# Attention pairs between the weight pieces of the second projections, heads normalised by token

## The chip, the cores and the metric

The kernel runs on one core of a Trainium2 chip. The metric is the device time in microseconds of one execution. A core has TensorE (PE in the profile, its weight loads PEld), VectorE (DVE), ScalarE (ACT), GpSimd (POOL) and SyncE (SP), which here issues all transfers. Each engine runs its own program in order; semaphores join them. The times before are 2862.55, 2863.42 and 2865.28 us.

## What is computed

Two transformer-like blocks on one sequence of 256 tokens with 2048 channels, in fp32. The change touches only the middle of the second block:

```
h = rms_norm(x, norm1_g)
aq, ak, av, bu, bg, cq, ck, cv = split(h @ w_in)      # 512 x 5, 1024, 128, 128 columns
aq, ak, cq, ck: rms_norm over each head's 64 channels, with a gain
out_a = dilated mixture of 3 banded attentions, 8 heads (q, k, v of A)
out_b = silu(layer_norm(causal conv over 31 taps of bu * sigmoid(bg)))
out_c = banded attention, window 128, 16 query heads on 2 key heads, with sinks
x = x + concat(out_a, out_b, out_c) @ w_out
x = x + (silu(rms_norm(x) @ w_gate) * (rms_norm(x) @ w_up)) @ w_down
```

All 256 tokens see one softmax per head: pattern A's three dilations are one masked softmax here, whose mask holds the logarithm of how many patterns reach a key. A pair is two heads on the partitions 0 to 63 and 64 to 127; there are 12, four of A and eight of C.

## The kernel before

Activations lie with the channels on the partitions: 16 tiles of 128 x 256. Every product with a weight matrix is split in fp32r: the weight is w_hi + w_lo, the input is x_hi (columns 0 to 255) and x_lo (256 to 511).

**Pieces and strips.** Weights come in pieces of 8 tiles of 128 x 128 (512 KB). Four pieces are a quad q. For each piece SP loads w_raw (one of 4 slots), ScalarE makes w_hi (`split`, L612), VectorE (slots 0 and 2, `lo`, L933) or GpSimd (slots 1 and 3, L1473) makes w_lo, and TensorE runs its matmuls, then increments pe_piece, which frees the slot. So the engines are at most four pieces ahead of TensorE. A strip (`strip`) makes 4 output tiles from 16 input tiles in 8 pieces: 8 matmuls w_hi by x_hi and x_lo (512 columns, L296), then 8 of w_lo by x_hi (256 columns, L300). Strips alternate between the PSUM groups GA and GB. ScalarE copies the x_lo half out (`halves`), VectorE adds the other (`total`, or `add_total` onto res).

`by_token` (L380 to L382) is the other form, used in the first block's merge: the input is stationary, the weights move, and the output has the tokens on the partitions.

**Second input projection.** Strips 138 and 140 make bu and bg, 142 to 148 aq, ak, av and half of cq, 150 the rest, and 152 (half a strip, 4 pieces) ck and cv, all into the tensor qkv. GpSimd multiplies each strip by the token's inverse root mean square (`scale_strip`, L1546). Beside 142 to 150 VectorE computes the convolution: 31 taps on each of four tiles (`taps2`, L1311), each tap reading the one before it on its tile.

**Attention.** TensorE stops taking pieces. It sums the squared heads (`head_sums`, L483), turns v to token rows (L490), turns the inverse norms of k (L510); VectorE scales k (L1360). Then per pair n: `scores` (L527, L528) into GA; VectorE `prepare` scales by q's norm, adds the mask (L1374), takes the peaks (L1379, L1380); ScalarE `exps` (L845, sinks L850); VectorE inverts the sum; GpSimd multiplies the probabilities by it (L1559); TensorE `transposes` (L539); ScalarE copies them (L863); `values` (L550, L551) gives channels by tokens; ScalarE and VectorE write x_hi and x_lo of the mixed tile (L858, L955). Scores run two pairs ahead. The convolution's layer norm stands between (two `column_sums`, L431).

**Output projection.** Four strips 153 to 159 with all 16 mixed tiles as input, added to res; behind each, the next input x2 is made (L775, L1273) and squared (L780). The following strip, 161, is the first of the gated block; `rms_beside` puts its sum of squares between its pieces.

Each engine's order is written by hand as a list of these calls, and the waits are on fixed counts.

## Time and profile before

| | us |
|---|---|
| three runs, lowest, median, highest | 2862.55, 2863.42, 2865.28 |
| the profiled execution | 2861.29 |
| its span, first to last instruction | 2859.5 |
| second input projection from strip 142 (44 pieces) | 149.8 |
| attention | 90.5 |
| output projection (32 pieces) | 91.5 |
| mean granted TensorE clock | 0.978 of full |

The span is 1.8 us shorter than the time of its execution. The page has the span in 40 slices of 71.5 us with a digit for each engine's busy share. A line of the timeline is: start, duration, engine, source line, operation, output<-input, partitions x elements, how many in a row, and in brackets how long the engine idled before and what released it.

### The profile page before, as it was taken

Reading aid. Unit: us, or ns where it says so; the run is one execution under the profiler, and the core shown is the slowest. Engines: PE = TensorE matmul, PEld = TensorE weight load, DVE = VectorE, ACT = ScalarE, POOL = GpSimd, SP = SyncE. Lnnn points to the kernel's source line nnn. Section 1 sums busy time; section 2 is a strip of 40 time slices with the busy share of each in tenths; the row PEclk is TensorE's granted clock in tenths of the full one; section 3 lists DMA queues with packets and bytes.
Section 4 is the critical chain, followed back from the end, with each engine's and each line's share of the span. In section 5 each row is a group of like instructions: output and inputs, shape, how many; then the busy total and the mean of one; then the engine's idle time right before and its main releaser. Section 6 shows DMA issues by size and latency. Waiting matters only on the chain.

```text
span 2859.5 us, 42940 instructions
## 1 busy us (share of the span) xinstructions
PE 2716.1 (95%) x15002; PEld 2355.0 (82%) x15002; DVE 1510.8 (53%) x1415; ACT 1361.7 (48%) x1527; POOL 1384.8 (48%) x588
## 2 busy tenths in 40 slices
PE   8999889999999899999999989886999999999999
PEld 7787777888888788888888878774888888888887
DVE  6676777222333544444444456986355455555455
ACT  5566655444444444444444444336444444444444
POOL 4566564444444444444444425454355555555554
PEclk9999999999999999999999999997999999999999
DMA  6444444556655355555555534440445555555554
GB/s 239 162 160 159 161 178 168 187 190 192 199 181 184 112 191 186 188 190 184 190 185 189 190 126 138 150 154 1 142 164 190 189 185 185 181 189 188 187 186 160
DMA packets 132280, 491.71 MB, mean 172 GB/s; under 512 B 14688, under 2 KB 14688, under 8 KB 132192
## 3 DMA queue, kind: packets, MB, share of 16 engines
q1 hardware_dynamic: 132192, 490.52, 51.6%
q8 instruction: 58, 0.95, 0.1%
q14 instruction: 30, 0.25, 0.0%
HBM read 488.36 MB, written 2.10 MB: 172 GB/s over the span
## 4 chain that ended last, share of the span: by engine, by line
PE 79%; DVE 10%; issue 4%; ACT 2%; POOL 2%; DMA 1%; DVEq 0%; ACTq 0%; SPq 0%; POOLq 0%
PE ps_b L296 21%; PE ps_a L296 20%; PE ps_b L300 11%; PE ps_a L300 11%; DVE w_lo L933 3%; DVE bconv L1311 2%; PE ps_a L380 2%; PE ps_a L381 2%; PE ps_a L382 2%; PE ps_b L380 2%; PE ps_b L382 2%; PE ps_b L381 2%; PE ps_a L431 1%; DMA w_raw<-w_dram 1%; ACT w_hi L612 1%
## 5 line engine op out<-in xcount | busy, mean ns | idle before, releaser
L1473 POOL TENSOR_TENSOR w_lo<-w_raw,w_hi 128x1024 fp32r<-128x1024 f32 (+1 forms) x454 | 1180.6, 2602 | 1337.8 <-ACT w_hi L612 1337.8
L612 ACT ACTIVATE w_hi<-w_raw 128x1024 fp32r<-128x1024 f32 (+1 forms) x908 | 972.3, 1076 | 1289.4 <-PE ps_b L300 437.1
L933 DVE TENSOR_TENSOR w_lo<-w_raw,w_hi 128x1024 fp32r<-128x1024 f32 (+1 forms) x454 | 698.9, 1540 | 939.2 <-ACT w_hi L612 936.9
L296 PE MATMUL ps_a<-xx,w_hi 128*128 128x512 f32 x1408 | 365.4, 402 | 23.8 <-DVE xx L955 9.3
L296 PE MATMUL ps_b<-xx,w_hi 128*128 128x512 f32 x1440 | 367.2, 397 | 13.6 <-ACT w_hi L612 10.1
L296 PEld LDWEIGHTS ps_a<-xx,w_hi 128*128 128x128 f32 x1408 | 261.1, 195 | 73.8 <-issue 20.8
L296 PEld LDWEIGHTS ps_b<-xx,w_hi 128*128 128x128 f32 x1440 | 263.6, 192 | 62.2 <-issue 11.3
L300 PEld LDWEIGHTS ps_a<-xx,w_lo 128*128 128x128 f32 x1408 | 197.8, 196 | 42.8 <-DVE w_lo L933 29.2
L300 PEld LDWEIGHTS ps_b<-xx,w_lo 128*128 128x128 f32 x1440 | 197.5, 192 | 40.1 <-DVE w_lo L933 26.7
L300 PE MATMUL ps_a<-xx,w_lo 128*128 128x256 f32 x1408 | 203.4, 289 | 25.4 <-DVE w_lo L933 25.4
L300 PE MATMUL ps_b<-xx,w_lo 128*128 128x256 f32 x1440 | 204.2, 285 | 22.2 <-DVE w_lo L933 22.2
L296 PE MATMUL ps_a<-ff,w_hi 128*128 128x512 f32 x864 | 216.3, 392 | 0.0
L296 PE MATMUL ps_b<-ff,w_hi 128*128 128x512 f32 x864 | 216.3, 392 | 0.0
L296 PE MATMUL ps_b<-x,w_hi 128*128 128x512 f32 x704 | 177.2, 393 | 3.6 <-DVE res L951 3.6
L296 PEld LDWEIGHTS ps_a<-ff,w_hi 128*128 128x128 f32 x864 | 155.4, 189 | 27.8
L296 PEld LDWEIGHTS ps_b<-ff,w_hi 128*128 128x128 f32 x864 | 155.3, 189 | 27.8
L296 PE MATMUL ps_a<-x,w_hi 128*128 128x512 f32 x704 | 177.2, 394 | 0.0
L296 PEld LDWEIGHTS ps_b<-x,w_hi 128*128 128x128 f32 x704 | 126.5, 189 | 28.0 <-issue 5.4
L296 PEld LDWEIGHTS ps_a<-x,w_hi 128*128 128x128 f32 x704 | 127.3, 190 | 22.9
L300 PEld LDWEIGHTS ps_b<-ff,w_lo 128*128 128x128 f32 x864 | 117.9, 190 | 8.4
L300 PEld LDWEIGHTS ps_a<-ff,w_lo 128*128 128x128 f32 x864 | 117.9, 190 | 8.4
L300 PE MATMUL ps_b<-ff,w_lo 128*128 128x256 f32 x864 | 120.5, 282 | 0.0
(244 smaller groups left out, 3440.2 us busy)
## 6 DMA issues: line engine op xcount, KB each, us to landing
w_raw<-w_dram SPq DMA_DIRECT2D x836, 512.0 KB, 3.3
w_raw<-w_dram SPq DMA_DIRECT2D x72, 640.0 KB, 4.2
zz<-x_dram SPq DMA_DIRECT2D x4, 512.0 KB, 6.9
out_dram<-res SPq DMA_DIRECT2D x4, 512.0 KB, 2.6
const<-const_dram SPq DMA_DIRECT2D x1, 449.0 KB, 10.4
prm<-prm_dram SPq DMA_DIRECT2D x1, 308.0 KB, 9.8
```

What stands on the lines that cost most here:

```text
L296: nc.tensor.matmul(group[:, j, :], w_hi[:, r, o * P:o * P + P], src[:, at + k, :], start=k == 0, stop=False)
L300: last = nc.tensor.matmul(group[:, j, 0:S], w_lo[:, r, o * P:o * P + P], src[:, at + k, 0:S], start=False, stop=k == kt - 1)
L380: nc.tensor.matmul(dst, x_hi, hi, start=k == 0, stop=False)
L381: nc.tensor.matmul(dst, x_hi, lo, start=False, stop=False)
L382: last = nc.tensor.matmul(dst, x_lo, hi, start=False, stop=k == kt - 1)
L431: last = nc.tensor.matmul(bank, ones[:, :], src[:, k, :], start=k == 0, stop=k == tiles - 1)
L612: act.activation(w_hi[:, r, 0:width], w_raw[:, r, 0:width], ACT.Copy).then_inc(hi_done, 1)
L933: dve.tensor_tensor(w_lo[:, r, 0:width], w_raw[:, r, 0:width], w_hi[:, r, 0:width].bitcast(F32), ALU.subtract).then_inc(lo_vec, 1)
L1311: ins = dve.scalar_tensor_tensor(y, x, column("cv_w", tile + 4 * (k0 + m)), y, ALU.mult, ALU.add)
L1473: pool.tensor_tensor(w_lo[:, r, 0:width], w_raw[:, r, 0:width], w_hi[:, r, 0:width].bitcast(F32), ALU.subtract).then_inc(lo_pool, 1)
```

## The change

The steps from quad 142 on are one list m = 0 to 59 of pieces (`Q0` = 142), and each engine calls a function `beside(m)` at each of them.

- The 44 pieces of the projection are `by_token` pieces: ck and cv first (m 0 to 3), cq (4 to 19), aq (20 to 27), ak (28 to 35), av (36 to 43). They go alternately to GB's two halves; SP fetches the pieces in that order. Only strips 138 and 140 (bu, bg) stay as they were, with GA and GB exchanged, and VectorE instead of GpSimd multiplies them by the token factor.
- Heads are normalised by token rows: ScalarE squares a group of heads from PSUM, VectorE sums and adds an eps that is scaled by the token's own square sum, ScalarE takes the root, VectorE multiplies, TensorE turns the tiles back, ScalarE keeps them (`head_squares` ... `keep_heads`). q's and k's token factors cancel in this. v is kept by token, scaled with tok_r.
- A pair starts every third piece from m = 16: `scores(n)` at m = 16 + 3n, `transposes` 2 pieces later, `values` 5, `turn_out` 6. C's eight pairs are first. Its GpSimd product is gone: `values` takes the raw exponentials as the stationary operand, gives tokens by channels, VectorE divides (`scale_out`), TensorE turns the result.
- The pairs use GA only; GB holds the pieces' sums. `prepare` is one addition of the mask.
- The taps are spread over m = 3 to 39: five in each step to 15, then five in two.
- The output projection's first two strips are 16 `narrow_piece`s at m = 44 to 59: matmuls of 256 columns, x_hi and x_lo one after the other into one half-bank, in an order of input tiles that follows the pairs. Strips 157 and 159 are ordinary.
- In a step ScalarE first splits piece m + 3, then calls, as far as due, values kept, the mixed tile's hi, `turned_probs`, `head_squares`, `keep_heads`, `exps`, `head_roots`. VectorE first makes the w_lo of piece m + 3 (in odd steps), then the mixed tile's lo, `scale_out`, `prepare`, `head_variance`, `norm_heads`, and the taps last.
- GpSimd has only its w_lo in these steps.

```diff
+        Q0 = 142
+        HEADS_END = (4, 12, 20, 28, 36)
+        V_END, MIX_AT = 44, 44
+        PAIRS_AT, EVERY = 16, 3
+        B_MEAN_AT, B_VAR_AT = 41, 47
+        def pair_at(m, late):
+            n, rest = divmod(m - PAIRS_AT - late, EVERY)
+            return n if rest == 0 and 0 <= n < len(PAIRS) else None
@@ TensorE @@
-            for n in range(16):
...
-                head_sums(n, squares[:, n, :])
...
+            def scores(n):
+                if n >= 1:
+                    pe.wait_ge(score_out, n)
+                if n >= 2:
+                    pe.wait_ge(o_scaled, n - 1)
...
             def transposes(n):
-                pe.wait_ge(p_ready, n + 1)
+                pe.wait_ge(exp_done, n + 1)
...
             def values(n):
...
+                    p_t = probs_t[:, n % 2, hd, :]
+                    nc.tensor.matmul(GA[:, 0, 64 * hd:64 * hd + 64], p_t[:, 0:P], vt[:, 0, v, part], start=True, stop=True)
+                    dst = GA[:, 0, P + 64 * hd:P + 64 * hd + 64]
+                    nc.tensor.matmul(dst, p_t[:, P:2 * P], vt[:, 0, v, part], start=True, stop=False)
+                    last = nc.tensor.matmul(dst, p_t[:, 2 * P:3 * P], vt[:, 1, v, part], start=False, stop=True)
+            def beside(m):
+                if m - 3 in HEADS_END:
+                    turn_heads(HEADS_END.index(m - 3))
+                n = pair_at(m, 2)
+                if n is not None:
+                    transposes(n)
+                n = pair_at(m, 5)
+                if n is not None:
+                    values(n)
+                n = pair_at(m, 6)
+                if n is not None:
+                    turn_out(n)
+                n = pair_at(m, 0)
+                if n is not None:
+                    scores(n)
...
+            by_token(Q0, GB[:, 2:4, :], xx, KT, nothing, nout=2, beside=beside)
+            by_token(Q0 + 1, GB[:, 0:2, :], xx, KT, nothing, beside=beside)
...
+            for m, (s, p) in enumerate(MIX_PIECES, MIX_AT):
+                beside(m)
...
+                narrow_piece(m, GB[:, 2 - 2 * s:4 - 2 * s, :], p)
+            strip(157, E_MIX + 2, GA, mix_tile, KT, nothing, free=lambda: pe.wait_ge(mix_lo, 12))
+            strip(159, E_MIX + 3, GB, mix_tile, KT, nothing, free=out_before(E_MIX + 3))
@@ ScalarE @@
+            def head_roots(x):
+                n = 8 if x else 2
+                act.wait_ge(head_var, x + 1)
+                act.activation(hsd[:, :, 0:n], hsum[:, :, 0:n], ACT.Sqrt).then_inc(head_sd, 1)
...
+            for m in range(MIX_END):
+                split(Q0 + (m + 3) // 4, (m + 3) % 4)
+                beside(m)
@@ VectorE @@
+            def taps_by(m):
+                return max(0, min(4 * TAPS2, 5 * (m - 2) if m < 16 else 65 + (5 * (m - 15) + 1) // 2))
...
+            for m in range(MIX_END):
+                if m % 2 == 1:
+                    lo(Q0 + (m + 3) // 4, (m + 3) % 4)
+                beside(m)
@@ GpSimd @@
-                scale_strip(i + E_IN2, qkv[:, ds(4 * i, 4), :])
...
-                        last = pool.tensor_scalar(probs[:, b, hd, cols], probs[:, b, hd, cols],
-                                                  rsum[:, b, hd, blk:blk + 1], None, ALU.mult)
...
+            with pool.Fori(0, 23) as i:
+                los(i + 139)
```

## Rows read from the trace of the kernel before

**Rows 1.** The page: busy time, slices, granted clock, and the chain by engine.
```profile
PE 2716.1 (95%) x15002; PEld 2355.0 (82%) x15002; DVE 1510.8 (53%) x1415; ACT 1361.7 (48%) x1527; POOL 1384.8 (48%) x588
...
PE   8999889999999899999999989886999999999999
...
PEclk9999999999999999999999999997999999999999
...
PE 79%; DVE 10%; issue 4%; ACT 2%; POOL 2%; DMA 1%; DVEq 0%; ACTq 0%; SPq 0%; POOLq 0%
```

**Rows 2.** Busy time by stage: us, then each engine's busy us, PEclk, DMA, GB/s.
```profile
1768.40:1918.20 149.80, 130.81 (x706) 112.40 (x705) 135.60 (x153) 55.38 (x53) 72.71 (x27) 0.95 0.42 150
1918.20:2008.70 90.50, 61.17 (x380) 45.26 (x379) 51.18 (x145) 52.59 (x153) 43.35 (x52) 0.76 0.07 25
2008.70:2100.20 91.50, 91.48 (x512) 80.35 (x513) 36.95 (x34) 42.60 (x49) 38.60 (x15) 0.98 0.52 168
```

**Rows 3.** Timeline of TensorE, input projection: start us, us, engine, line, what, [idle before].
```profile
1768.44 2.00 PE L296 MATMUL ps_a<-xx,w_hi 128*128 128x512 f32 x8
1770.28 1.11 PE L300 MATMUL ps_a<-xx,w_lo 128*128 128x256 f32 x8
1771.23 2.00 PE L296 MATMUL ps_a<-xx,w_hi 128*128 128x512 f32 x8
...
1815.10 1.96 PE L300 MATMUL ps_b<-xx,w_lo 128*128 128x256 f32 x8 [4.59 <-DVE w_lo L933]
1816.86 2.86 PE L296 MATMUL ps_b<-xx,w_hi 128*128 128x512 f32 x8
```

**Rows 4.** Timeline of all engines, input projection beside the taps.
```profile
1790.81 1.21 DVE L933 TENSOR_TENSOR w_lo<-w_raw,w_hi 128x1024 fp32r<-128x1024 f32 x1
...
1792.18 2.50 POOL L1473 TENSOR_TENSOR w_lo<-w_raw,w_hi 128x1024 fp32r<-128x1024 f32 x1 [3.16 <-ACT w_hi L612]
...
1792.60 2.37 DVE L1311 SCALAR_TENSOR_TENSOR bconv<-bpad,prm,bconv 128x256 f32<-128x256 f32 x1 [0.18 <-DVE bconv L1311]
...
1795.81 2.07 DVE L1311 SCALAR_TENSOR_TENSOR bconv<-bpad,prm,bconv 128x256 f32<-128x256 f32 x5 [0.18 <-DVE bconv L1311]
```

**Rows 5.** Timeline of TensorE, by-token pieces of the merge stage.
```profile
526.61 0.39 PE L380 MATMUL ps_b<-w_hi,xx 128*128 128x512 f32 x1
...
529.33 0.39 PE L380 MATMUL ps_b<-w_hi,xx 128*128 128x512 f32 x1
```

**Rows 6.** Timeline of all engines, attention, around the ninth to twelfth pair.
```profile
1992.78 0.50 PE L527 MATMUL ps_a<-qkv 64*128 64x128 f32 x4
...
1993.75 0.66 PE L550 MATMUL ps_b<-probs_t,vt 128*64 128x256 f32 x4
...
1994.23 0.40 PE L551 MATMUL ps_b<-probs_t,vt 128*64 128x128 f32 x4
...
1996.46 0.87 PE L539 MATMUL ps_b<-const,probs 128*128 128x128 f32 x6 [1.84 <-POOL probs L1559]
...
1998.08 0.39 ACT L845 ACTIVATE probs<-probs,negm 128x128 f32<-128x128 f32 x1
...
1999.83 0.47 ACT L850 ACTIVATE sink<-negm,prm 128x2 f32<-128x2 f32 x2
```

**Rows 7.** Timeline of TensorE, start of the attention: the head sums.
```profile
1918.22 4.23 PE L483 MATMUL ps_b<-const,squares 128*128 128x2 f32 x32
```

**Rows 8.** Groups of VectorE instructions by line and form: xcount, busy us, mean ns.
```profile
L1380 DVE TENSOR_REDUCE peak<-probs 128x2 f32<-128x512 f32 x12 | 8.1, 676 | 0.0
...
L1379 DVE TENSOR_REDUCE peak<-probs 128x2 f32<-128x256 f32 x12 | 5.0, 420 | 0.4
```

**Rows 9.** Timeline of all engines, first strip after the output projection.
```profile
2118.93 2.08 PE L300 MATMUL ps_a<-x,w_lo 128*128 128x256 f32 x8 [5.52 <-DVE w_lo L933]
...
2125.71 1.28 ACT L784 ACT_TABLE_LOAD   x1
...
2127.01 0.47 ACT L784 ACTIVATE rms<-ps_b,eps 128x256 f32<-128x256 f32 x1
```

More of the change, by code:

```diff
@@ L27 @@
 E_IN2 = E_MLP + 48
-E_MIX = E_IN2 + 8
+E_MIX = E_IN2 + 2
 E_FF2 = E_MIX + 4
@@ L209, in build @@
+        score_psum, score_out, peak_ready, exp_done = (
+            sem(n) for n in ("score_psum", "score_out", "peak_ready", "exp_done"))
+        pt_psum, pt_out, o_psum, o_scaled, o_turned = (
+            sem(n) for n in ("pt_psum", "pt_out", "o_psum", "o_scaled", "o_turned"))
+        mix_hi, mix_lo = sem("mix_hi"), sem("mix_lo")
         sq_summed = sem("sq_summed")
         b_hi, b_lo = sem("b_hi"), sem("b_lo")
-        rms_ready, qkv_made = sem("rms_ready"), sem("qkv_made")
+        rms_ready = sem("rms_ready")
@@ L839, in exps @@
+            splits(141)
+            splits(142, N8, (0, 1, 2))
+            halves(E_IN2 + 1, 4 * 142, GA)
             def exps(n):
@@ L1357, in _ @@
[L1357 to L1363 removed]
+            dve.wait_ge(tok_root, 1)
+            own.done(dve.reciprocal(tok_r[:, :, :], tok_sd[:, :, :]))
@@ new lines, in _, with taps @@
+            los(142)
+            total(E_IN2 + 1, GA, bug[:, 4:8, :])
+            by_rms(bug[:, 4:8, :]).then_inc(bg_made, 1)
+            tap_of = [None] * 4
+            def taps(first, last):
+                for n in range(first, last):
+                    k, tile = divmod(n, 4)
+                    y, x = bconv[:, tile, :], bpad[:, tile, k:k + S]
+                    if k == 0:
+                        ins = dve.tensor_scalar(y, x, column("cv_w", tile), column("cv_b", tile), ALU.mult, ALU.add)
+                    else:
+                        own.need(tap_of[tile])
+                        ins = dve.scalar_tensor_tensor(y, x, column("cv_w", n), y, ALU.mult, ALU.add)
+                    if k == TAPS2 - 1:
+                        ins.then_inc(b_made, 1)
+                    else:
+                        tap_of[tile] = own.done(ins)
@@ new lines, in beside @@
+            def beside(m):
+                n = pair_at(m, 6)
+                if n is not None:
+                    lo_of(mixed(n)[:, S:2 * S], GA[:, 2, 0:S], mixed(n)[:, 0:S], n + 1, mix_hi, mix_lo)
+                n = pair_at(m, 5)
+                if n is not None:
+                    scale_out(n)
+                n = pair_at(m, 0)
+                if n is not None:
+                    prepare(n)
+                if m in HEADS_END:
+                    head_variance(HEADS_END.index(m))
+                if m - 1 in HEADS_END:
+                    norm_heads(HEADS_END.index(m - 1))
+                if m == 2:
+                    dve.wait_ge(bg_sig, 1)
+                    own.need()
+                    own.done(dve.tensor_tensor(bpad[:, :, 30:30 + S], bug[:, 0:4, :], bug[:, 4:8, :], ALU.mult))
+                    own.need()
+                taps(taps_by(m - 1), taps_by(m))
+                if m == B_MEAN_AT:
+                    dve.wait_ge(b_mean, 1)
+                    dve.tensor_tensor(bconv[:, :, :], bconv[:, :, :], each_token(bmean), ALU.subtract).then_inc(b_cent, 1)
+                if m == B_VAR_AT:
```

594 lines of the change are left out of this document (310 added, 284 removed).

## The prediction

> **What bounds the kernel now.** I read the page first: TensorE is busy 95% of the span, and the chain that ended last is 79% TensorE [rows 1]. The digits of the 40 slices show one hole, a 6 with a granted clock of 7; it is the 28th slice, 1930 to 2001 us. Then the windows, cut where the stages change [rows 2]: the second input projection of 44 pieces (1768.4 to 1918.2), the attention (90.5 us, TensorE busy 61.2, clock 0.76), and the output projection of 32 pieces (91.5 us). The change rewrites these three, 331.8 us of the 2859.5. Everything else is a chain of pieces of 8 weight tiles, one each 2.79 us (starts 1768.44 and 1771.23) [rows 3]. So TensorE's own work bounds both projections, and the attention, which has no pieces, is bounded by a chain from engine to engine. The projection is not clean either: 149.8 us against 44 x 2.79 = 122.8. TensorE idled 19.0 of it (149.80 less 130.81 busy [rows 2]), in waits for VectorE's w_lo, the longest 4.6 us [rows 3], and after each the next pieces run slower (2.86 for 2.00 us).
>
> **Why VectorE is late there.** It holds the taps of the 31-tap convolution. Five taps take 2.07 us, 0.41 each, a w_lo 1.21; a tap that meets GpSimd's w_lo (2.50 us) takes 2.37, nearly as long as the other engine's instruction [rows 4]. So while VectorE has taps to do, each GpSimd instruction adds some 2.1 us to it (2.50 less what is over by then). The change takes eight scalings and 48 small products off GpSimd, and packs the taps closer. The Trainium skill ("SBUF — State Buffer", section "SBUF: two separate sides") calls this an exclusive lock between GpSimd and VectorE instructions with two SBUF inputs; the trace agrees, 2.37 us for a tap of 0.48. If engines only shared bandwidth, the wait at step 18 below would shrink by 14 us.
>
> **The sum, part by part, TensorE first.** 76 pieces before are 76 after; no weight traffic is added, and SP issues the transfers in another order, each still behind the same buffer waits: no cost. The 60 steps m = 0 to 59 stand for pieces 142 to 156, then 16 pieces of two ordinary strips.
> Projection, now by token: 12 matmuls of 512 columns start 2.72 us apart (526.61 to 529.33) [rows 5], so 40 pieces are 108.8; the first four have 24 matmuls of 256 columns. the lower half of a strip's piece has 8 such in 0.95 us (1770.28 to 1771.23) [rows 3], so 2.85 a piece, 11.4. Sixteen narrow pieces have the same 24 matmuls: 45.6. Two strips: 16 x 2.79 = 44.7.
> Attention on TensorE: scores 0.95 us (the group begins at 1992.78, the values follow at 1993.75), six transposes 0.87 [rows 6]. The values change form: six matmuls with a 128x128 stationary and 64 columns, in fp32, so 12 instructions. Bounds: 0.88 as before (1993.75 to 1994.63) [rows 6], and 12 x 0.132 = 1.6 by the nearest row of full weight loads with almost no columns, 32 in 4.23 us [rows 7]. I take 1.6, since weight loads dominate. Two turning transposes 0.3, gaps at the four changes 0.5. Together 4.2 x 12 = 50.5.
> Turning the heads: 34 transposes x 0.145 = 5.0. Sums for the convolution's norm, 16 instructions of 256 columns as before, by the values' four such in 0.66 [rows 6] 2.6 and two gaps: 3.0. Zero matmuls 4 x 0.23 = 0.9. Sums by token, 16 instructions x 0.132 = 2.1.
> All of TensorE: 120.2 + 45.6 + 44.7 + 50.5 + 5.0 + 3.0 + 0.9 + 2.1 = 272.0. With no wait at all the change would save 331.8 - 272.0 = 59.8 us. Gone are the head sums, the turning of v, the k rows, and GpSimd's products, for which TensorE waits between exps and transposes (1.84 us ahead of the group at 1996.46 [rows 6]); what is late next follows.
>
> **What the waits give back.** First, m = 0 to 18. Taps start only when the sigmoid has come: ScalarE reaches it in step 2, after piece 1 (5.6 us), then split 1.06, table load 1.28, sigmoid 1.06, VectorE's product 1.2: 10.4 us after the first by-token piece starts. Then five taps stand in each step up to 15. Two steps cost VectorE 10 x 0.415 + 1.21 + 2.1 for GpSimd's lock = 7.5, so 13 steps are 48.6, and the first two head groups (reduce of 1024 elements and product at 1.2 each, small ones 0.4) add 4.7. Step 16 begins at 63.7. Its prepare, 2.4 us (768 elements at the w_lo's rate 0.9, the reductions 0.42 and 0.68 [rows 8], two small 0.4), lets exps(0) start at 66.1; exps with its sinks is 2.2 us (1998.08 to 2000.30 [rows 6]), so it ends at 68.4 with the semaphore. In program order TensorE's transposes(0) stand in front of piece 18 and wait for it; behind them are all matmuls, and with their pe_piece the splits, the los and SP's next transfers; by its own work (11.4 + 14 x 2.72 + 1.5 heads + 1.1 scores) it is there at 52.1. Wait: 16.3. A wait this long slows the next pieces, as behind the 4.6 us [rows 3]: 2.5.
> Second, each pair. Measured from the end of piece m-1, scores end at 1.6, piece m at 4.4, ScalarE's next split at 5.5, exps at 7.7; TensorE is at the transposes at 7.1. Wait 0.6, twelve times, 7. Where ScalarE has something in front of exps it is later: head squares at step 20, turned heads and a table load at 23, table loads at 32, 38 and 50, values kept at 44. At 1.1 to 2.3 each, 8. Together 15. The head roots' table loads cost 1.28 us each, and the next instruction starts when the load ends (2125.71 to 2127.01) [rows 9]. The Trainium skill ("ScalarE: Activation LUTs", "What ACT_TABLE_LOAD costs") counts 2.66 us for a switch with its drain; the trace shows no drain. By that rule the five late ones would cost some 7 us more; I leave it out.
> Is VectorE fast enough there? A round of three pieces has 1.5 w_lo 1.8, 7.5 taps 3.1, prepare 2.4, scale_out 1.1, lo 0.4, heads 1.1, lock 1.5 x 2.1 = 3.2: 13.1 us. TensorE's round is 8.2 + 4.2 + 0.5 heads + 1.1 wait = 14.0. TensorE still sets it, by 0.9, so I take no cost; this is the thinnest margin of the working.
> After the last mix piece nothing changes: the 5.5 us wait in the following strip [rows 9] has its x2, its sums and its GpSimd order as before, and I keep it. VectorE's own scalings of bug (2.5 us) lie in the strip before, where it waits some 4 us a w_lo.
>
> **Forecast.** 272.0 + 16.3 + 2.5 + 15 = 305.8 against 331.8: 26.0 us less. The profiled execution took 2861.3 (span 2859.5 and 1.8 around it), giving 2835.3; the median of the three runs is 2.1 above it, so I predict **2837.4**.
>
> **Rivals.**
> *VectorE sets the rounds* (18%). Its 13.1 us has no waits in it, and it waits in order for o_psum, mix_hi and score_psum. Three such waits of 1 us make 16; 2.1 more than TensorE's round, in the eight rounds with taps, 17: 2854. For it: VectorE was busy 135.6 of 149.8 us in this stage [rows 2]. Against: those waits fall where it has slack.
> *VectorE is not late at step 16* (16%). If GpSimd's lock catches few taps, since w_lo on GpSimd itself waits, the 18.8 vanish: 2819. Against: it caught nearly all in [rows 4]. The low end adds the pair waits gone and values at 0.88: 2863.4 - 59.8 + 4 = 2808.
> *The clock falls in every round* (12%), the case on the slow side. Small fp32 matmuls and a wait for exps stand between two pieces in 14 rounds; if they bring the clock from its 2.4 to its 1.2 GHz level, the small ones take 1.5 to 2 us longer and the piece behind them 1.7 (1.96 + 2.86 for 1.11 + 2.00 [rows 3]), 3.0 a round, 42 in all: 2879. It decides from 1.9 a round. For it: clock 0.76 in the attention [rows 2]. Against: there TensorE stood idle a third of the time, here 0.6 us a round. The Trainium skill ("TensorE: Matmul & The Clock Gate", "Part 4: PE-mode transpose") says that transposes don't count as busy, which speaks for this case; no row here separates them.
> *It doesn't do what it says* (2%): some wait orders the pairs behind the pieces; then only the values' and products' time moves: about 2860.
> The forecast's own case has 52%.
>
> **Range and chances.** 2808 to 2860 leaves out the clock case, the last one and the edges, under 2 in 10. A measurement tells 0.2% (5.7 us) from no change. Faster: 52 + 16 + 13 of the 18, 0.81. Same 0.06. Slower 0.13.
>
> **What would show it.** By-token pieces 2.72 apart; narrow pieces 2.85 (right) or over 3 (weight loads bound them); values 1.6 or 0.9. A wait of TensorE ahead of transposes(0), some 10 us long, ended by exps, with VectorE without a gap before it. Then rounds of 14 us with short waits ended by ACTIVATE; if VectorE sets them, it has no idle time and TensorE waits for w_lo or o_scaled. Clock 0.95 or more from m = 18 on; under 0.9 is the clock case. Wrong would also be a stage that is long because straight-line code arrives late, which no row of before prices.

## The result

The changed kernel took **2833.07 us** (median; 2832.35 to 2834.90) beside 2863.86 us for the kernel before on the same chip: ratio 0.9893, 95% interval 0.9876 to 0.9910, 30.8 us less. 2837.4 was predicted, within 2808 to 2860. So the time is right to 4.3 us. Several of its terms are not, and they cancelled; the runs below show which.

The page of the kernel after, the lines that answer to [rows 1] (busy time; slices of TensorE and its clock; the chain by engine):

```profile
PE 2710.8 (96%) x15030; PEld 2356.6 (83%) x15030; DVE 1484.0 (52%) x1398; ACT 1370.7 (48%) x1540; POOL 1324.7 (47%) x532
...
PE   8999889999999899999999998889999999999999
...
PEclk9999999999999999999999999999999999999999
...
PE 82%; DVE 9%; ACT 4%; issue 3%; POOL 1%; DMA 1%; ACTq 0%; DVEq 0%; SPq 0%; POOLq 0%
```

The hole is gone: no slice of TensorE's busy share is under 8, and none of its clock under 9. TensorE's busy time hardly fell (2716.1 to 2710.8 us), the span by 28.2. The windows, cut at the first piece by tokens, the first transposes, the ninth transposes, the end of the narrow pieces, the end of the two strips, and behind the next long wait (us, then the engines' busy us; PEclk, DMA share, GB/s), against [rows 2]:

```profile
1770.36:1838.50 68.14, 55.47 (x284) 46.03 (x282) 63.46 (x98) 30.33 (x42) 25.62 (x9) 0.95 0.44 150
1838.50:1952.80 114.30, 104.67 (x530) 84.19 (x531) 76.64 (x143) 64.16 (x134) 28.97 (x12) 0.93 0.32 109
1952.80:2025.40 72.60, 69.93 (x540) 66.36 (x538) 29.25 (x46) 37.06 (x60) 21.57 (x9) 0.98 0.38 123
2025.40:2070.10 44.70, 44.70 (x258) 39.34 (x257) 23.08 (x24) 25.37 (x32) 19.55 (x8) 1.00 0.57 187
2070.10:2100.00 29.90, 23.88 (x120) 20.55 (x119) 19.47 (x10) 12.42 (x15) 17.92 (x7) 0.89 0.40 139
```

VectorE is full in the first window (63.5 of 68.1 us) and has room in the second (76.6 of 114.3). The output projection ends at 2070.10, before it was 2100.2.

TensorE's timeline of the kernel after, all but the pieces' own instructions left out (start, us, engine, line, what, idle time before and its releaser):

```profile
1806.60 0.47 PE L431 MATMUL ps_b<-w_hi,xx 128*128 128x512 f32 x1 [2.10 <-DVE w_lo L1079]
...
1823.70 1.97 PE L541 MATMUL ps_b<-const,hnb 128*128 128x128 f32 x8 [6.87 <-DVE hnb L1537]
...
1838.56 0.98 PE L574 MATMUL ps_a<-const,probs 128*128 128x128 f32 x6 [2.04 <-ACT sink L925]
...
1882.10 0.88 PE L574 MATMUL ps_a<-const,probs 128*128 128x128 f32 x6 [0.64 <-ACT sink L925]
1882.81 0.33 PE L588 MATMUL ps_a<-vt,probs_t 128*128 128x64 f32 x2
...
1894.45 0.88 PE L574 MATMUL ps_a<-const,probs 128*128 128x128 f32 x6 [0.62 <-ACT sink L925]
```

The transposes of the first pair begin 68.2 us after the first piece by tokens (68.4 predicted). From then to the last pair's transposes pass 155.6 us, and 95.1 more to the end of the next long wait, which is the 6.03 us for w_lo in the following strip (5.52 in [rows 9]). These three stretches are called **early part**, **rounds** and **rest** below. All that lies ahead of them is the same in every kernel, but it varied by up to 6 us from one profiled execution to the next, so the stretches tell more than the spans do.

| kernel | early part | rounds | rest | sum | median of the runs |
|---|---|---|---|---|---|
| before (the whole stage) | | | | 350.5 | 2863.9 |
| after | 68.2 | 155.6 | 95.1 | 318.9 | 2833.1 |
| no_taps | 54.1 | 153.0 | 95.2 | 302.3 | 2817.3 |
| vec_lo | 62.7 | 152.1 | 96.7 | 311.5 | 2827.1 |
| even_taps | 59.1 | 149.3 | 96.7 | 305.1 | 2821.8 |
| exps_first | 65.9 | 146.7 | 93.9 | 306.5 | 2821.9 |
| no_roots | 68.2 | 143.8 | 96.7 | 308.7 | 2823.5 |
| filler | 68.2 | 148.0 | 93.6 | 309.7 | 2824.4 |
| exps_vec | 60.6 | 145.3 | 93.9 | 299.8 | 2816.7 |
| early_fixed | 54.6 | 149.8 | 93.9 | 298.3 | 2814.9 |
| out_first | 54.6 | 145.5 | 93.6 | 293.8 | 2809.6 |
| apart | 144.1 | 121.2 | 120.9 | 386.3 | 2902.2 |
| apart_ahead | 144.4 | 87.8 | 119.3 | 351.5 | 2863.6 |

All kernels of the table but no_taps and no_roots compute the whole of the reference. Each kernel's runs stood beside runs of the kernel before, whose medians lay between 2863.5 and 2864.7; ratios are to those.

### The profile page after: what moved, and what is told of

It is laid out like the page before. It is cut to its first block, busy times and chain, and to the rows that moved or that the text cites. A ratio compares the mean times of both kernels' runs of the same rounds, so it can differ in the third digit from the quotient of the medians.

```text
span 2831.3 us, 42416 instructions
## 1 busy us (share of the span) xinstructions
PE 2710.8 (96%) x15030; PEld 2356.6 (83%) x15030; DVE 1484.0 (52%) x1398; ACT 1370.7 (48%) x1540; POOL 1324.7 (47%) x532
## 4 chain that ended last, share of the span: by engine, by line
PE 82%; DVE 9%; ACT 4%; issue 3%; POOL 1%; DMA 1%; ACTq 0%; DVEq 0%; SPq 0%; POOLq 0%
PE ps_b L345 21%; PE ps_a L345 20%; PE ps_b L349 11%; PE ps_a L349 10%; PE ps_b L431 3%; PE ps_b L432 3%; PE ps_b L433 3%; DVE w_lo L1079 3%; PE ps_a L431 2%; PE ps_a L432 2%; PE ps_a L433 2%; ACT w_hi L711 1%; DVE bconv L1475 1%; PE ps_a L482 1%; PE ps_b L659 1%
## 5 line engine op out<-in xcount | busy, mean ns | idle before, releaser
L1079 DVE TENSOR_TENSOR w_lo<-w_raw,w_hi 128x1024 fp32r<-128x1024 f32 (+1 forms) x454 | 687.7, 1516 | 953.2 <-ACT w_hi L711 951.4
L345 PE MATMUL ps_b<-xx,w_hi 128*128 128x512 f32 x1184 | 305.8, 401 | 23.2 <-DVE xx L1103 9.5
L345 PE MATMUL ps_a<-xx,w_hi 128*128 128x512 f32 x1120 | 286.2, 398 | 13.1 <-DVE xx L1103 9.3
L345 PEld LDWEIGHTS ps_b<-xx,w_hi 128*128 128x128 f32 x1184 | 218.8, 194 | 64.5 <-issue 19.1
L345 PEld LDWEIGHTS ps_a<-xx,w_hi 128*128 128x128 f32 x1120 | 204.7, 192 | 51.6 <-issue 9.7
L349 PEld LDWEIGHTS ps_b<-xx,w_lo 128*128 128x128 f32 x1184 | 165.3, 195 | 32.7 <-DVE w_lo L1079 21.3
L349 PE MATMUL ps_b<-xx,w_lo 128*128 128x256 f32 x1184 | 170.3, 288 | 18.1 <-DVE w_lo L1079 18.0
L349 PEld LDWEIGHTS ps_a<-xx,w_lo 128*128 128x128 f32 x1120 | 154.5, 193 | 23.1 <-DVE w_lo L1079 12.4
L349 PE MATMUL ps_a<-xx,w_lo 128*128 128x256 f32 x1120 | 158.5, 285 | 10.7 <-DVE w_lo L1079 10.7
L431 PE MATMUL ps_b<-w_hi,xx 128*128 128x512 f32 (+1 forms) x320 | 127.0, 397 | 3.6 <-DVE w_lo L1079 3.6
```

The source lines that it names most:

```text
L345: nc.tensor.matmul(group[:, j, :], w_hi[:, r, o * P:o * P + P], moving(src, at + k), start=k == 0, stop=False)
L349: last = nc.tensor.matmul(group[:, j, 0:S], w_lo[:, r, o * P:o * P + P], moving(src, at + k)[:, 0:S], start=False, stop=k == kt - 1)
L431: nc.tensor.matmul(dst, x_hi, hi, start=k == 0, stop=False)
L1079: dve.tensor_tensor(w_lo[:, r, 0:width], w_raw[:, r, 0:width], w_hi[:, r, 0:width].bitcast(F32), ALU.subtract).then_inc(lo_vec, 1)
```

## Experiments

### What makes the early part long

The prediction had VectorE late at step 16, because of the taps and of GpSimd's w_lo beside them. Three kernels test that: one without taps, one that takes GpSimd's w_lo away from beside them, one that spreads them.

**no_taps.**

```diff
                     k, tile = divmod(n, 4)
+                    if 0 < k < TAPS2 - 1:
+                        continue
```

> The changed kernel with taps 1 to 29 of the 31 left out (116 of 124 tap instructions), so pattern B's output is not the convolution's; all waits and all other work stay. The question: what do the taps cost now? Theory (VectorE is full only up to step 16): the waits ahead of the first turned heads and the first transposes (2.1 + 1.5 + 6.9 + 2.0 us before 1838.56) and the slow pieces behind them go, so the first transposes start near 1770.4 + 52 instead of 68 us; the rounds of three pieces stay near 14 us, since TensorE sets them and ScalarE's exps set the short waits. In all 14 to 18 us faster, 2815 to 2819. Rival (VectorE sets the rounds): the eight rounds from 1838.5 to 1952.8 shrink from 14.3 to 13 us or less each as well, another 10 us or more: 2809 or less. Rival (the early waits come from ScalarE or the transfers, not from the taps): under 5 us faster.

Measured: 2817.32 us, ratio 0.9830 (0.9814 to 0.9847), 15.8 us faster than the change. The early part fell by 14.1 us to 54.1, TensorE's waits in it from 12.7 to 2.0. The rounds lost 2.6. So the taps cost ahead of the first transposes and hardly behind them: the rival that VectorE sets the rounds has no support.

**vec_lo.** The six early w_lo go from the engine that disturbs to the engine that is disturbed.

```diff
                 if m % 2 == 1:
                     lo(Q0 + (m + 3) // 4, (m + 3) % 4)
+                elif 2 <= m <= 12:
+                    dve.wait_ge(lo_pool, 2 * (Q0 + (m + 3) // 4) + (m + 3) % 4 // 2)
+                    lo(Q0 + (m + 3) // 4, (m + 3) % 4, done=lo_pool)
```

(`lo` is given the semaphore that it increments, and GpSimd's list leaves these six out)

> The changed kernel, but the w_lo of six of GpSimd's pieces in the first steps (made in steps 2, 4 to 12) is made by VectorE; nothing is left out. VectorE gets 6 x 1.2 = 7.2 us of new work and loses six meetings with a GpSimd instruction. Theory (a GpSimd w_lo beside taps costs VectorE nearly its whole 2.1 us): VectorE gains 6 x (2.1 - 1.2) = 5.4 us by step 16, and the first transposes start about that much earlier: 4 to 7 us faster, 2826 to 2829. Rival (the engines only share bandwidth, or VectorE's late steps come from its own waits): VectorE gets later by up to 7 us: 2 to 8 us slower, 2835 to 2841.

Measured: 2827.14 us, ratio 0.9869 (0.9853 to 0.9885). The intervals of this kernel and of the change overlap, so 5.9 us by the medians is not sure by itself; the trace gives the mechanism. The early part is 5.5 us shorter (5.4 expected), though VectorE got 7.2 us more to do. (The rounds are 3.5 us shorter too, as the clock did not fall behind the first pair's wait of 2.04 us and fell less behind the sixth's; more on this below.) The cause stands in VectorE's and GpSimd's timeline of the kernel after:

```profile
1813.62 2.06 DVE L1475 SCALAR_TENSOR_TENSOR bconv<-bpad,prm,bconv 128x256 f32<-128x256 f32 x5
1815.60 1.21 DVE L1524 TENSOR_REDUCE hsum<-hsq 128x16 f32<-128x1024 f32 x1
1816.84 0.17 DVE L1527 TENSOR_TENSOR hsum<-hsum,eps_d 128x16 f32<-128x16 f32 x1
1816.94 4.15 DVE L1475 SCALAR_TENSOR_TENSOR bconv<-bpad,prm,bconv 128x256 f32<-128x256 f32 x5
1821.01 1.21 DVE L1079 TENSOR_TENSOR w_lo<-w_raw,w_hi 128x1024 fp32r<-128x1024 f32 x1
1822.14 0.24 DVE L1533 RECIPROCAL hrn<-hsd 128x16 f32<-128x16 f32 x1
1822.42 1.22 DVE L1537 TENSOR_TENSOR hnb<-ps_b,hrn 128x1024 f32<-128x1024 f32 x1
...
1818.37 2.43 POOL L1651 TENSOR_TENSOR w_lo<-w_raw,w_hi 128x1024 fp32r<-128x1024 f32 x1 [9.67 <-ACT w_hi L711]
```

Five taps take 2.06 us alone and 4.15 with one GpSimd w_lo of 2.43 beside them: 2.1 us added, as taken from [rows 4]. It also shows the order in which VectorE works off step 12 and 13: five taps, a w_lo, and only then the heads' product (hnb), for which TensorE waits 6.87 us. There is no gap ahead of it; VectorE is late, not waiting.

**even_taps.**

```diff
-                return max(0, min(4 * TAPS2, 5 * (m - 2) if m < 16 else 65 + (5 * (m - 15) + 1) // 2))
+                return max(0, min(4 * TAPS2, (4 * TAPS2 * (m - 2) + 36) // 37))
```

> The changed kernel with the same 124 taps spread evenly, 3.35 in each step from 3 to 39, instead of 5 in each step up to 15 and 2.5 after; nothing is left out. Up to step 16 VectorE then has 23 taps fewer, 10 to 15 us by 0.415 to 0.64 us each; the rounds of three pieces have 2.5 taps more, 1.0 to 1.6 us. Theory (VectorE, busy 76.6 of 114.3 us in the rounds, has room there, and only what lies ahead of step 16 costs): the 12.5 us of early waits and the slow pieces behind them mostly go, the rounds stay at 14.3: 10 to 15 us faster, 2818 to 2823. Rival (the prediction's count of 13.1 us for VectorE's round against TensorE's 14.0 is right): the rounds become VectorE's and grow by 0.2 to 0.9 each, and half of the gain is gone: 2824 to 2830.

Measured: 2821.78 us, ratio 0.9852 (0.9836 to 0.9868), 11.3 us faster. The early part is 59.1 us. The rounds fell from 155.6 to 149.3, because the clock stayed up behind three waits where it had fallen (and fell behind one, of 1.52 us, where it had not); but intervals at the same clock have the same length with 2.5 more taps in them (the fourth 12.36 for 12.35 us, the fifth 15.86 for 15.75). So VectorE's spare time in a round is well above the 0.9 us of the prediction's count.

### What makes the rounds long

TensorE's own work in a round is 11.7 us (three pieces of 8.16 in all and 3.6 of pair, worked out below; out_first has rounds of 11.51 without a wait), but eleven intervals took 155.6, 14.1 each. Two causes were in question: what stands ahead of exps on ScalarE, and the clock. The timeline of the kernel after (VectorE's last instruction for the pair, then ScalarE), ahead of the third pair's transposes, which wait 2.03 us:

```profile
1860.81 0.22 DVE L1501 TENSOR_SCALAR negm<-peak,prm 128x2 f32<-128x2 f32 x1
...
1861.93 1.00 ACT L950 ACTIVATE cqt<-ps_b 128x1024 f32<-128x1024 f32 x1
...
1862.96 1.28 ACT L920 ACT_TABLE_LOAD   x1
...
1864.25 0.40 ACT L920 ACTIVATE probs<-probs,negm 128x128 f32<-128x128 f32 x1
...
1866.02 0.47 ACT L925 ACTIVATE sink<-negm,prm 128x2 f32<-128x2 f32 x2
```

VectorE's peaks were there at 1861.0; ScalarE kept the turned heads and loaded its table first, and exps began 3.2 us later.

**exps_first.**

```diff
             for m in range(MIX_END):
+                if pair_at(m, 1) is not None:
+                    exps(pair_at(m, 1))
                 split(Q0 + (m + 3) // 4, (m + 3) % 4)
                 beside(m)
```

(and the call in `beside` is taken out)

> The changed kernel with ScalarE's exps of a pair ahead of, instead of behind, the split and copies of the same step; nothing is left out. Theory (what TensorE waits for ahead of the transposes is ScalarE's split of 1.06 us, and what else it does in front of exps; the clock falls behind the waits of 2 us): the twelve waits, 13.4 us in all, shrink to 3 to 6 us, and the slow rounds behind three of them (15.7 and 15.5 instead of 13.3) come back: 8 to 15 us faster, 2818 to 2825. Rival one (VectorE's prepare is what exps waits for, in the same step): exps can't start earlier, and the split that now stands behind it comes later: no change to 5 us slower. Rival two (the low clock comes from the transposes and the small fp32 matmuls, not from the waits): only the waits' share, 5 to 9 us faster, with the granted clock of 1838 to 1953 still at 0.93.

Measured: 2821.87 us, ratio 0.9852 (0.9836 to 0.9869), 11.2 us faster; the rounds lost 8.9. Ahead of the transposes TensorE now waits five times for ScalarE, 5.0 us in all. The granted clock of 1838 to 1953 is 0.99. Both rivals fall: exps could start earlier, and the clock came back with the waits.

**no_roots.**

```diff
-                act.activation(hsd[:, :, 0:n], hsum[:, :, 0:n], ACT.Sqrt).then_inc(head_sd, 1)
+                act.activation(hsd[:, :, 0:n], hsum[:, :, 0:n], ACT.Copy).then_inc(head_sd, 1)
```

> The changed kernel with the root left out of the heads' normalisation: ScalarE copies where it took the root, so the output of patterns A and C is wrong in scale. With the root the engine's two function tables stop changing at the head groups, some five loads of 1.28 us at the groups and as many back to the exponential. Theory (the loads stand in front of exps at three or four pairs, and the clock falls behind the 2 us waits they make): the waits ahead of the transposes lose 1.3 us at three or four pairs, and one or two slow rounds of +2 to +3 us go: 5 to 9 us faster, 2824 to 2828. Rival (the loads hide beside the pieces; the pair waits come from the split and the copies alone): under 2 us.

Measured: 2823.51 us (2820.74 to 2828.92), ratio 0.9855 (0.9838 to 0.9871): 9.6 us by the medians. The early part is the same, the rounds are 11.8 us shorter, more than expected. The third and the sixth wait fell from 2.03 and 2.04 to 0.60 and 0.62, 2.9 us in all, and the intervals behind them from 15.6 to 12.4 each, 6.4. Two of these intervals of 15.6 had the clock at 0.78, now it is up: a table load of 1.28 us that lengthens such a wait costs more than its own length.

**filler.** Does idling lower the clock, or do the small fp32 matmuls and transposes? The order of the waits is changed and seven matmuls stand ahead of the wait for exps:

```diff
             def transposes(n):
-                pe.wait_ge(exp_done, n + 1)
                 if n >= 1:
                     pe.wait_ge(pt_out, n)
                 if n >= 2:
                     pe.wait_ge(mix_lo, n - 1)
+                if n in (0, 2, 5, 11):
+                    for _ in range(7):
+                        nc.tensor.matmul(GA[:, 2, 0:P], ones[:, :], ident, start=True, stop=True)
+                pe.wait_ge(exp_done, n + 1)
```

> The changed kernel with seven matmuls more (a matrix of ones by 128 columns, some 0.2 us each by the convolution's sums, 1.5 us together) ahead of TensorE's wait for exps at the first, third, sixth and last pair, those where it idles 1.85 to 2.04 us; their result is overwritten, and nothing is left out. The wait ends at the same time, but TensorE has worked through most of it. Theory (idling is what lowers the clock): the wait shown shrinks to 0.3 to 0.7 us, and the intervals behind the third and sixth pair, 15.6 us at a clock of 0.78, fall to 12.4 to 13 as behind the short waits, the first from 13.3 to 11.7, and the slow piece behind the last (3.66 us) goes: 7 to 9 us less in the stage, 2824 to 2826. Rival (the small fp32 matmuls and transposes lower the clock, or the clock is late by its own rhythm): no change or, since the added matmuls may outlast the wait, up to 2 us more: 2831 to 2835.

Measured: 2824.38 us (2819.82 to 2826.56), ratio 0.9859 (0.9843 to 0.9876): 8.7 us faster by adding work. The ratio's interval just touches the change's (0.9876 to 0.9910), but all four times lie under the change's lowest, 2832.35. Windows of the kernel after, from the second to the seventh pair's transposes, by pairs (columns as above; the figure behind the last count is the clock):

```profile
1851.86:1866.54 14.68, 12.65 (x72) 10.18 (x73) 11.07 (x25) 10.09 (x20) 2.41 (x1) 1.00 0.40 143
1866.54:1882.10 15.56, 14.92 (x65) 12.22 (x65) 7.74 (x13) 6.30 (x16) 4.39 (x2) 0.78 0.22 68
1882.10:1894.45 12.35, 11.73 (x64) 9.36 (x65) 10.22 (x22) 7.18 (x17) 2.73 (x2) 1.00 0.40 127
1894.45:1910.20 15.75, 12.84 (x72) 10.21 (x72) 14.24 (x23) 10.10 (x20) 4.82 (x2) 1.00 0.31 103
1910.20:1925.81 15.61, 14.93 (x65) 12.06 (x65) 8.56 (x20) 6.34 (x16) 2.40 (x1) 0.78 0.28 101
```

and of filler, with its added matmuls in the second view:

```profile
1853.49:1868.17 14.68, 14.17 (x86) 11.88 (x87) 10.99 (x25) 9.99 (x20) 2.40 (x1) 1.00 0.42 144
1868.17:1880.62 12.45, 11.75 (x64) 9.38 (x65) 8.38 (x14) 6.36 (x16) 4.48 (x2) 1.00 0.25 84
1880.62:1893.05 12.43, 11.72 (x64) 9.36 (x65) 10.19 (x21) 7.18 (x17) 3.02 (x2) 1.00 0.40 128
1893.05:1908.70 15.65, 14.36 (x87) 11.91 (x87) 14.15 (x23) 10.02 (x20) 4.84 (x2) 1.00 0.32 104
1908.70:1921.15 12.45, 11.74 (x64) 9.38 (x65) 8.60 (x20) 6.36 (x16) 2.40 (x1) 1.00 0.37 125
```

```profile
1865.94 1.72 PE L572 MATMUL ps_a<-const,ones 128*128 128x128 f32 x14
1868.17 0.87 PE L577 MATMUL ps_a<-const,probs 128*128 128x128 f32 x6 [0.51 <-ACT sink L928]
```

The interval that holds the wait is as long as before (14.68 and 14.68), since the wait still ends when exps end. The one behind it falls from 15.56 to 12.45 us, its clock from 0.78 to 1.00. Its own instructions are the same in both kernels.

One kernel could have been lucky: in even_taps the clock stayed at 1.00 behind waits of 2.04, 2.06 and 2.04 us with nothing to fill them. So I read the granted clock of the 5 us behind every wait of 0.5 us or more, from 1800 to 2010 us, in the ten profiles of kernels with interleaved pairs. Behind the 33 waits of over 1.7 us it was under 0.8 in 25 and 1.00 in 8: it fell behind all nine of 2.5 us or more, and behind 16 of the 24 between 1.7 and 2.1. Behind the 74 shorter ones it was 1.00 in 73 and 0.66 once (1.52 us, in even_taps). So the transposes and small matmuls, which stand behind most of those 74, do not lower it by themselves, and filler shows that without the long idling it stays up. But the length of the wait alone doesn't decide.

Nor does the work around the wait. Ahead of two sums of squares, in parts of the program that no kernel here changes, TensorE waits 2.82 us in each of the 14 profiles, 28 times in all. In the 5 us behind, the clock was under 0.8 in 12 and 1.00 in 16. The first of the two, in the kernel after and in no_taps:

```profile
953.00:958.00 5.00, 4.96 (x23) 4.39 (x24) 2.30 (x3) 3.18 (x3) 0.00 (x0) 1.00 0.00 0
953.00:958.00 5.00, 4.58 (x15) 3.85 (x16) 2.68 (x3) 3.53 (x4) 0.00 (x0) 0.67 0.00 0
```

So idling makes a fall possible and does not make it sure, and the stretches of a single profile, such as the rounds of vec_lo and even_taps, can hold a share of 1.5 to 3.2 us a wait that the edit did not make. What decides between falling and not stays open.

### Do the repairs add up, and is there a better version?

**exps_vec** is exps_first and vec_lo together.

> The changed kernel with two of the three edits: exps ahead of the split and six early w_lo on VectorE; the taps stay as the change has them. From the first piece by tokens to the first transposes it should take 66 - 5.5 = 60 us, the eleven intervals of pairs 146.7 as with exps ahead alone (149.8 with the evenly spread taps too), and the rest 93.9. Theory (the edits add up, since one acts ahead of the first transposes and the other behind): 2815 to 2817. Rival (an earlier start of the pairs brings back waits that the late start hid): 2819 to 2822.

Measured: 2816.66 us (2813.77 to 2819.72), ratio 0.9830 (0.9814 to 0.9847). Early part 60.6, rounds 145.3, rest 93.9, nearly as expected (60, 146.7, 93.9): they add up, each in its own stretch.

**early_fixed** adds the evenly spread taps to these two.

> The changed kernel with three edits together: exps ahead of the split, VectorE making six of GpSimd's early w_lo, and the taps spread evenly; nothing is left out. Alone the first gave 11.2 us and the second 5.9. Theory (the first acts on the waits of the rounds, the other two both on the same 12.5 us of early waits, so these two don't add up): 11 for the rounds and 12 to 15 for the early part, 23 to 27 us faster than the changed kernel, 2806 to 2810. Rival (with the waits of ScalarE gone, VectorE's rounds, 2.5 taps fuller, become the bound): 2812 to 2820, with waits of TensorE ended by VectorE's scaled output and w_lo in the rounds.

Measured: 2814.91 us, ratio 0.9827 (0.9811 to 0.9843), 18.2 us faster than the change: the rival's range, not the theory's. Beside exps_vec, which differs by the taps alone, that is 1.8 us by the medians, and the intervals of the two overlap. The early part did what was expected, 54.6 us with one wait of 2.6 left. But the rounds are 149.8 against exps_first's 146.7 and exps_vec's 145.3, so they give back 4.5 of the 6.0 us that the early part gained over exps_vec. TensorE waits in them five times for VectorE's scaled output, 5.3 us, the longest 1.94. With ScalarE out of the way VectorE is next, and there the taps that were moved behind step 16 count.

**out_first** puts VectorE's part of the pairs ahead of its w_lo.

```diff
             for m in range(MIX_END):
+                n = pair_at(m, 5)
+                if n is not None:
+                    scale_out(n)
+                n = pair_at(m, 0)
+                if n is not None:
+                    prepare(n)
                 if m % 2 == 1:
                     lo(Q0 + (m + 3) // 4, (m + 3) % 4)
```

(and the calls in `beside` are taken out)

> The version with the three edits (exps ahead of the split, six early w_lo on VectorE, taps spread evenly), and now VectorE's scaling of a pair's output and its addition of the mask stand ahead of, instead of behind, the w_lo of 1.2 us of the same step; nothing is left out. In the version without this edit TensorE waits five times, 5.3 us in all, for the scaled output, the longest 1.94 us with a slow round of 16.2 behind it. Theory (the w_lo stands in front of it at every second pair): these waits go, and a slow round with them, 5 to 9 us: 2806 to 2810. Rival (VectorE is simply full in those rounds): the wait moves to the w_lo behind, no gain: 2813 to 2817.

Measured: **2809.61 us** (2809.02 to 2812.36), ratio 0.9811 (0.9795 to 0.9828). By the medians the 5.3 us came. The interval overlaps early_fixed's, but the stage is 4.5 us shorter and the rounds are 145.5. How they came is not quite as expected: TensorE still waits four times for the scaled output, 4.8 us, but no longer than 1.63, and behind none of them the clock falls. In the 114.30 us from the first transposes (1827.56 to 1941.86) VectorE is busy 102.74 us and the clock is 0.99. It is the fastest version of this study, 23.5 us under the change and 54.6 under the kernel before.

### What is the interleaving itself worth?

The change does two things: cheaper links in the pairs' chain (no product on GpSimd, heads by token), and pieces between them. Three kernels take them apart.

**no_product**, from the kernel before:

```diff
-                for hd in range(2):
-                    for blk, cols in ((0, slice(0, P)), (1, slice(P, 3 * P))):
-                        last = pool.tensor_scalar(probs[:, b, hd, cols], probs[:, b, hd, cols],
-                                                  rsum[:, b, hd, blk:blk + 1], None, ALU.mult)
-                last.then_inc(p_ready, 1)
+                pool.tensor_scalar(rsum[:, b, 0, 0:1], rsum[:, b, 0, 0:1], 1.0, None, ALU.mult).then_inc(p_ready, 1)
```

> The kernel before with GpSimd's product of the probabilities left out (one instruction of one column stands for the four of each pair), so its attention is not normalised; pieces and pairs stay apart. It measures what that one removal is worth where nothing is interleaved. TensorE waits 1.84 us for the product ahead of a group of transposes, at some ten pairs, at a low clock. Theory (the product was one link of a chain that bounds the attention, and dropping it shortens the 90.5 us by 1.5 to 2.5 us a pair): 18 to 28 us faster than before, 2836 to 2846, so most of what the whole change gained could be had by this alone. Rival (another wait, for exps or the copies, stands right behind it): under 8 us faster, 2856 or more, and the gain of the change is the interleaving's.

Measured: 2847.93 us, ratio 0.9941 (0.9924 to 0.9957), 16.8 us faster than before, just short of the theory's 18. TensorE's waits ahead of the transposes fell from 21.3 us (nine) to 6.3 (two), but those for the turned probabilities rose from 4.5 to 8.6: part of the wait stood right behind.

**apart**: the changed kernel with the pairs in a stage of their own, steps 44 to 83, which have no pieces (piece 44 follows at step 84).

```diff
-        V_END, MIX_AT = 44, 44
+        V_END, MIX_AT = 44, 84
...
-        PAIRS_AT, EVERY = 16, 3
-        B_MEAN_AT, B_VAR_AT = 41, 47
+        PAIRS_AT, EVERY = 44, 3
+        B_MEAN_AT, B_VAR_AT = 69, 75
...
+            for m in range(44, 84):
+                beside(m)
```

> The changed kernel with the interleaving undone and the rest kept: heads by token, values with the exponentials as the stationary operand, no GpSimd product. The twelve pairs run as a stage of their own between the 44th and the 45th piece, with nothing beside them but the rest of the taps' order; nothing is left out. Then a round has 4.2 us of TensorE's work and the chain prepare, exps, scale and turn is bare. Theory (the chain of a pair, about 8 us in the kernel before, is hidden by pieces now): the stage takes 12 x 7 to 12 x 8 us = 84 to 96 instead of the 50 us of TensorE's own work that the pairs cost interleaved; the wait at the first transposes (16 us) goes, as nothing stands there. In all +18 to +45 us, 2851 to 2878: the interleaving is worth more than the whole gain. Rival (the gain comes from the cheaper pairs and heads themselves, and the interleaving gives back in waits what it hides): within 8 us of the changed kernel, 2825 to 2841.

Measured: 2902.21 us, ratio 1.0127 (1.0110 to 1.0144): outside what either theory gave, 24 us above the higher. One pair of it, TensorE's timeline:

```profile
1940.63 1.54 PE L577 MATMUL ps_a<-const,probs 128*128 128x128 f32 x6 [4.78 <-ACT sink L930]
1941.97 0.53 PE L591 MATMUL ps_a<-vt,probs_t 128*128 128x64 f32 x2
...
1945.20 0.69 PE L601 MATMUL ps_a<-const,on 128*128 128x128 f32 x2 [0.57 <-DVE on L1522]
1945.82 0.81 PE L564 MATMUL ps_a<-ckt,cqt 64*128 64x128 f32 x4
1946.41 1.07 PE L565 MATMUL ps_a<-ckt,cqt 64*128 64x256 f32 x4
1952.25 1.54 PE L577 MATMUL ps_a<-const,probs 128*128 128x128 f32 x6 [4.77 <-ACT sink L930]
```

A pair takes 11.62 us, and everything in it is in one chain: in the order that the change wrote for steps with pieces, the next scores stand behind this pair's values, so nothing of the next pair is under way. The idling also keeps the clock down: 0.56 over the rounds, and the six transposes take 1.54 us for 0.87. I had taken the chain from the kernel before, where scores run two pairs ahead.

**apart_ahead**: the same with the next scores ahead of the transposes.

```diff
-                n = pair_at(m, 2)
+                n = pair_at(m, 4)
...
-                if n >= 2:
-                    pe.wait_ge(mix_lo, n - 1)
+                if n >= 1:
+                    pe.wait_ge(mix_lo, n)
...
-                pe.wait_ge(pt_out, min(n + 2, 12))
+                pe.wait_ge(pt_out, n + 1)
```

> The version with the pairs in a stage of their own again, but with the scores of the next pair ahead of this pair's transposes, so that VectorE's and ScalarE's part of the next pair runs beside TensorE's part of this one; nothing is left out. In the version before this one each pair took 11.6 us, as all its steps stood in one chain, 4.8 us of it TensorE's wait for exps. Theory (that order, and not the pairs themselves, cost more than expected, and a chain with the next scores ahead is bounded by TensorE's 4.2 us of work at the low clock, 7 or so, with some 1 to 2 us for the copy and the scaling): 8 to 9 us a pair, 30 to 43 less: 2859 to 2872, at or above the kernel before's time, so that the interleaving is worth 26 to 39 us. Rival (the exponentials still end last): 10.5 or more a pair, over 2885.

Measured: 2863.61 us, ratio 1.000 (0.9991 to 1.0010); a pair takes 8.0 us. That is the time of the kernel before. The clock of its rounds is 0.64, in the kernel after it is 0.95. Here all of the heads by token and the pairs without a product are in place, and they bring nothing: whatever the product's 16.8 us would give is used up, by the values in fp32 with the exponentials as weights, the scaling and turning behind them, scores only one pair ahead, or the packed taps (its 44 pieces still have 14.3 us of waits); these were not told apart. The 30.5 us between this kernel and the change is what the interleaving is worth over this order of the pairs, the clock included. It is no bound for every order: no_product, where scores run two pairs ahead, is only 14.9 us slower than the change, but it leaves the division out, and no run here has heads by token with the pairs apart and scores two ahead.

## Why the prediction was right, and where not

**Pieces.** By token 2.72 us (1784.62 to 1787.34), narrow 2.88 (2013.89 to 2016.77; 2.85 predicted), and of the first four 2.88. Right; weight loads do not bound the narrow ones.

**A pair on TensorE: mis-sized.** 4.2 us was predicted. The interval of 12.35 us (1882.10 to 1894.45) is three pieces, 8.16, a wait of 0.62 and 3.6 us of pair. The transposes take 0.71 from start to start, not 0.87, which is a duration with its end; the twelve value matmuls 1.26 (1852.57 to 1853.83), between the bounds 0.88 and 1.6 of which I took the upper. Eleven pairs in the rounds: 6.9 us too much.

**The early part: right time, wrong place.** VectorE is what is late, by the lock on the taps, and the first transposes start at 68.2 for 68.4. The prediction has one wait of 16.3 us, ahead of the transposes. In the trace it is 2.10, 1.52, 6.87 and 2.04 us, and the largest is at the turned heads of step 15, which TensorE takes from VectorE before it comes to the first pair; the sum had no wait there. At the turned heads of step 7 it had waited 0.20. TensorE's own time to the transposes was put at 52.1; in out_first, with 2.6 us of waits left, they start at 54.6, so it is 52.0.

**The Trainium skill on the lock.** The prediction leaned on "SBUF — State Buffer", section "SBUF: two separate sides". The row of 4.15 us for 2.06 agrees with an exclusive lock, and vec_lo shows what follows from it: the engine that is short of time gains by doing the other's work itself.

**The pair waits: right cause and size.** 15 us predicted for twelve, 13.4 measured, ended by ScalarE in all but one of 0.67, for which the profile names no engine; 0.62 and 0.64 where only the split is in front (0.6 predicted), 0.8 to 2.0 where heads, values or a table load are too; at two pairs none. exps_first and no_roots confirm both parts.

**The clock behind them: the missing term.** The sum charged one slowdown of 2.5 us, behind the first transposes' wait, and none behind the other pairs. Behind the pairs' four waits of 1.85 to 2.04 us it fell each time, and filler, which removes just this, is 9.2 us shorter in its stage. Yet the rival "the clock falls in every round" was wrong too: behind 0.6 us waits the clock is 1.00 with all the transposes. The rule of the Trainium skill that the prediction named for it ("TensorE: Matmul & The Clock Gate", "Part 4: PE-mode transpose", transposes don't count as busy) did not decide here: six transposes, two turning ones and twelve small matmuls in each interval left the clock at 1.00 wherever the waits were short.

**The ledger.** Early part 68.4 predicted, 68.2 measured. Rounds: 26 pieces by token 70.7, seven narrow 20.0, eleven pairs 46.2, heads, sums and zero matmuls 6.9, waits 14.4, clock 2.5: 160.7 predicted, 155.6 measured. Cheaper pairs (-6.9) and shorter waits (-2.2) and a dearer clock (about +5.5, from the two slow intervals and the first) account for -3.6 of the -5.1. Then 74.6 predicted (305.8 less these two and the 2.1 of the token sums, which lie ahead) and 75.9 measured to the end of the strips, of which 1.5 is the slow piece behind the last wait. In all 4.0 us under the forecast, as the medians say (4.3). That it is no more is partly luck, since two misses cancelled: the pairs came out 6.9 us cheaper and the clock 5.5 dearer, and neither was foreseen.

**VectorE's round: wrong.** I counted 13.1 us against TensorE's 14.0 and gave 18% to VectorE setting the rounds. Measured, it is busy 76.6 us in eight rounds, 9.6 each. A tap's mean in them is 620 ns with the lock in it, and the lock met fewer of them than I charged: 4 of the 51 taps took over 1 us, where the count had 12 meetings in eight rounds. even_taps put 2.5 taps more into each round without lengthening those at the same clock; early_fixed, with ScalarE's waits gone, shows that they do cost there, and out_first's 102.7 of 114.3 us come near the margin that I had feared.

**The rivals.** "VectorE not late at step 16" fell with no_taps. "It doesn't do what it says" fell with apart_ahead, where the pairs stand behind the pieces, and which is 30.5 us slower.

## What to carry to other kernels

When work is put between the bound engine's pieces, price each point where that engine takes something from another by two numbers: the wait, and what its clock loses behind it. Here a wait of 0.6 us cost itself, and the four of 1.85 to 2.04 us cost 3.4 to 5.2 each; the cheap repair is the order on the helper engine, the result that the bound engine waits for ahead of bulk work (11 us for moving one call on ScalarE). Look for each hand-over in and right behind a stretch in which a helper is overfull, since the lag shows there (here 10.5 of 12.7 us) and not only where the new work begins.

And measure the parts of a change apart in an order that suits them: the first such version here was 39 us slower than the second, because scores no longer ran ahead.

## What the runs showed of the hardware

- TensorE's granted clock was down behind 25 of 33 waits of over 1.7 us and behind 1 of 74 of 0.5 to 1.7, all in the changed stage of ten kernels. Behind one and the same wait of 2.82 us elsewhere it was down 12 times of 28. At the lower of its two levels (1.2 GHz; 2.4 otherwise) the six transposes take 1.54 us for 0.87. Seven matmuls on constants ahead of each of four waits kept it up, for 8.7 us of the kernel's time.
- A GpSimd w_lo of 2.43 us beside five taps on VectorE adds 2.1 us to their 2.06.
- Small fp32 matmuls, 128x128 stationary and 64 columns, start 0.105 us apart (twelve in 1.26), and with 128 columns 0.111 (the fourteen of filler).
- A switch of ScalarE's function table is 1.28 us, with the next instruction right behind (1862.96 and 1864.25).
